# A two-layer DeltaNet and Mamba-2 decode step on one core: regrouped side work, castings in other places, norms by logarithm and exponential

## The reference, cut to what matters

```python
DEPTH = 2    # layer 0: gated DeltaNet (GDN), layer 1: Mamba-2 SSD; D_MODEL = 2048, f32 throughout
for i in range(DEPTH):
    hn = rmsnorm(h, norm_w[i])
    h = h + mixer_i(hn)                   # in-projection, causal conv, SiLU, chunked scan, gate, out-projection
    e = rmsnorm(p[i] @ W_proj_i, ple_norm_w[i])
    h = h + e * sigmoid(h @ W_gate_i)     # "ple"
y = rmsnorm(h, final_norm_w)

def l2norm(x):                            # GDN: on q and k, per head of 128
    return x * rsqrt(sum(x * x) + EPS)
# GDN per head pair: A = I + strict lower part, inverted; u, w, qk; state S (128 x 128) over chunks
# sample tokens, per sequence b: kv = k_t S_b ; o = q_t S_b   ("readout" of the 8 cached states)
# SSD per group: cb = C B^T, y_diag, y_off from the state, S = decay * S + B^T x
```

## Time and profile before

| | |
|---|---|
| median of 3 runs | 2591.24 us (2588.82 to 2592.79) |
| profiled execution, its own time | 2590.68 us |
| its span | 2588.9 us, so 1.8 us lie around it |
| PE, PEld busy | 94%, 87% |
| POOL, DVE, ACT busy | 67%, 58%, 46% |
| mean granted clock of TensorE | 0.98 |

### The profile page before, as it was taken

The page is one execution under the profiler, slowest core; times in us unless marked ns, Lnnn a source line. Parts: engine busy times, 40 slices in busy tenths (PEclk is TensorE's granted clock), DMA queues, the critical chain, the costliest instruction groups (busy, mean ns, idle before and its releaser), DMA issues.

```text
span 2588.9 us, 58121 instructions
## 1 busy us (share of the span) xinstructions
PE 2439.7 (94%) x21088; PEld 2262.6 (87%) x21088; DVE 1491.2 (58%) x2978; ACT 1181.6 (46%) x2116; POOL 1734.7 (67%) x2236
## 2 busy tenths in 40 slices
PE   5999999999999999999998989999999999999887
PEld 4889888888888888889998879988898888899887
DVE  7555665555656556562114457888888888611434
ACT  4444444444444444443334346454545455433433
POOL 4455555555555555556797768877887777889776
PEclk9999999999999999999999989999999999999989
DMA  5344444334333343434443336655576546454433
GB/s 193 137 147 140 145 139 147 123 134 139 127 129 129 139 145 139 139 133 169 147 163 135 136 140 228 230 182 184 199 237 207 184 169 220 176 175 156 141 123 125
DMA packets 126772, 410.83 MB, mean 159 GB/s; under 512 B 21345, under 2 KB 37985, under 8 KB 122113
## 3 DMA queue, kind: packets, MB, share of 16 engines
q1 hardware_dynamic: 81216, 295.75, 33.0%
q10 hardware_dynamic: 45504, 114.38, 13.1%
HBM read 363.47 MB, written 46.61 MB: 158 GB/s over the span
## 4 chain that ended last, share of the span: by engine, by line
POOL 59%; issue 37%; PE 3%; POOLq 1%; DVE 0%; ACT 0%; DVEq 0%; ACTq 0%
POOL wl L327 59%; PE psj L350 1%; PE psj L352 1%; PE psj L351 1%; POOLq L331 0%; POOLq L325 0%; DVE h L1940 0%; DVE arena L1938 0%; ACT L1150 0%; POOLq L327 0%; ACT arena L1125 0%; PE psA L374 0%; ACT arena L1333 0%; DVE arena L1410 0%; DVEq L139 0%
## 5 line engine op out<-in xcount | busy, mean ns | idle before, releaser
L327 POOL TENSOR_TENSOR wl<-ring,wh 128x256 fp32r<-128x256 f32 x2232 | 1734.5, 811 | 832.5 <-ACT wh L801 829.9
L350 PE MATMUL psj<-xh,wh 128*128 128x288 f32 x4400 | 1376.3, 313 | 74.9 <-POOL wl L327 33.7
L351 PE MATMUL psj<-xl,wh 128*128 128x288 f32 x4400 | 1312.7, 298 | 0.0
L352 PE MATMUL psj<-xh,wl 128*128 128x288 f32 x4400 | 1307.5, 297 | 0.0
L350 PEld LDWEIGHTS psj<-xh,wh 128*128 128x128 f32 x4400 | 838.0, 190 | 143.7 <-issue 62.9
L351 PEld LDWEIGHTS psj<-xl,wh 128*128 128x128 f32 x4400 | 840.8, 191 | 5.4 <-issue 4.4
L352 PEld LDWEIGHTS psj<-xh,wl 128*128 128x128 f32 x4400 | 841.9, 191 | 0.0
L801 ACT ACTIVATE wh<-ring 128x1024 fp32r<-128x1024 f32 x558 | 575.2, 1056 | 530.6 <-PE psj L352 464.3
L872 ACT ACTIVATE arena<-psj 128x256 f32<-128x256 f32 x112 | 42.6, 381 | 265.9 <-PE psj L352 265.9
L1766 DVE SCALAR_TENSOR_TENSOR arena<-arena 128x256 f32<-128x256 f32 x144 | 124.2, 902 | 2.6
L1699 DVE TENSOR_TENSOR h<-h,psj 128x288 f32 x32 | 14.5, 454 | 173.7 <-PE psj L352 173.7
(11 more groups left out here) (345 smaller groups left out, 2895.0 us busy)
## 6 DMA issues: line engine op xcount, KB each, us to landing
ring<-weights_d SPq DMA_DIRECT2D x558, 512.0 KB, 3.3
h<-gstate_d ACTq DMA_DIRECT2D x16, 1024.0 KB, 4.8
gst_s_d<-h ACTq DMA_DIRECT2D x16, 1024.0 KB, 4.6
h<-sstate_d ACTq DMA_DIRECT2D x32, 512.0 KB, 5.4
sst_s_d<-h ACTq DMA_DIRECT2D x32, 512.0 KB, 6.0
arena<-g_rows_d ACTq DMA_DIRECT2D x16, 864.0 KB, 4.2
arena<-s_rows_d ACTq DMA_DIRECT2D x8, 1152.0 KB, 8.0
h_spill_d<-h ACTq DMA_DIRECT2D x2, 2304.0 KB, 8.0
```

The lines of the kernel that those rows point to most:

```text
L327: ins = pool.tensor_tensor(wl[:, s, n:n + 2], ring[:, s, n:n + 2], wh[:, s, n:n + 2].bitcast(F32), ALU.subtract)
L350: pe.matmul(out, w_h, xh[:, kt, :], start=(kt == 0), stop=False)
L351: pe.matmul(out, w_h, xl[:, kt, :], start=False, stop=False)
L352: mm = pe.matmul(out, w_l, xh[:, kt, :], start=False, stop=(kt == KT - 1))
```

## The change

It has many parts. In groups:

1. **GDN norms of q and k.** `gdn_norm` sums the squares by a product with ones that leaves the sum on every partition (two matmuls of 288 columns, into psA and psB). ScalarE then takes the logarithm (L912, L913) and the exponential of -0.5 times it (`g_qk_roots`), and VectorE multiplies by that. `gdn_scale` and the reciprocals are gone. The output norm (`OR`) is made in the same way.
2. **Sample work of the GDN heads on four tiles.** The readout writes k and q products of both value heads into four column groups of 32, 128 columns each, where it wrote two groups of 256. `us`, `osm`, `esp`, the copies and norms behind follow that layout.
3. **Fewer breaks.** GDN: `us` joins e = 23, `osm` and `gdn_norm` join e = 27, `esp` goes to e = 15, and the wait for `g_bs` goes from unit 14 to 15. SSD: `s_tok` at 20, chunk state 0 and readout at 32, `s_off`, chunk state 1, `s_smp` and chunk output 0 at 34, chunk output 1 and transposes at 44, states at 49 and 59. That is seven breaks for eleven.
4. **VectorE's order.** The taps of the v convolution are put in smaller pieces between the steps of the inversion. In the SSD group y1 and the state go ahead of the sample chain.
5. **ScalarE's order.** Castings move at the starts of the dense stages. In `ple` a tile is cast one tile earlier, and the squares run one later. In the SSD group the SiLU of the sample columns goes behind `decays(0)`.
6. **The beginning.** Inputs are issued from two queues, and the squares no longer wait for `prm`.

```diff
             def gdn_norm(m):
                 pe.wait_ge(S("g_sq"), m + 1)
-                for n in range(2):
-                    for c in range(NC):
-                        pe.matmul(psB[:, 2 * n + c:2 * n + c + 1], gSQ[:, n, c * CH:(c + 1) * CH], ones[:, 0:1],
-                                  start=True, stop=True)
...
+                for n, bank in enumerate((psA, psB)):
+                    mm = col_sum(bank[:, 0:T], gSQ[:, n, :])
                 mm.then_inc(S("g_ss"), 1)
-            def gdn_scale():
...
                     for b in range(DEC_B):
                         for n in range(2):
-                            mm = pe.matmul(psD[NS * n:NS * n + NS, 0:2 * P], (gMK, gMQ)[n][:, b, :], gS[:, b, :, :],
-                                           start=(b == 0), stop=(b == DEC_B - 1))
+                            for j in range(2):
+                                at = NS * (2 * n + j)
+                                mm = pe.matmul(psD[at:at + NS, 0:P], (gMK, gMQ)[n][:, b, :], gS[:, b, j, :],
+                                               start=(b == 0), stop=(b == DEC_B - 1))
...
+                if e == 32:
+                    pe.wait_ge(S("s_btc"), m + 1)
+                    chunk_state(0)
                     pe.wait_ge(S("s_pr"), m + 1)
...
-            def split_x(src, n, t0):
+            def split_x(src, n, t0, first=False, second=False):
+                if first:
+                    upper(0, 0, 2 * t0 + 2)
                 if t0:
                     act.wait_ge(half_done, 2 * t0)
                 for kt in range(n):
+                    if second and kt == n // 2:
+                        upper(0, 0, 2 * t0 + 3)
                     act.activation(xh[:, kt, :], src(kt), ACT.Copy).then_inc(xh_ready, 1)
...
+            for n in (1, 3):
+                act.dma_start(h[:, 4 * n:4 * n + 4, :], x_in[:, 4 * n:4 * n + 4, :]).then_inc(S(f"x_in{n}"), 16)
...
+                act.activation(gSQ[:, 0, :], psA[:, 0:T], ACT.Ln, bias=eps_c)
+                act.activation(gSQ[:, 1, :], psB[:, 0:T], ACT.Ln, bias=eps_c).then_inc(S("g_nc"), 1)
+            def g_qk_roots(m):
+                act.wait_ge(S("g_nc"), m + 1)
+                act.activation(gSQ[:, :, :], gSQ[:, :, :], ACT.Exp, scale=-0.5).then_inc(S("g_rn"), 1)
...
-                act.activation(ga["OR"], ga["OS"], ACT.Sqrt, bias=eps_c, scale=1.0 / P).then_inc(S("g_rs2"), 1)
+                act.activation(ga["OR"], ga["OS"], ACT.Ln, bias=eps_c, scale=1.0 / P).then_inc(S("g_ol"), 1)
+                act.wait_ge(S("g_ol"), m + 1)
+                act.activation(ga["OR"], ga["OR"], ACT.Exp, scale=-0.5).then_inc(S("g_rs2"), 1)
+                if full:
+                    g_qk_roots(m + 1)
...
             def ple(tp, te, es, hq, hbase, td, end):
                     if i == 7:
                         ahead(0, 0, te)
+                    if i == 13:
+                        upper(0, 0, 2 * te + 2)
...
                 gate(0, 0)
+                ahead(0, 0, te + 3)
                 gate(0, 1)
...
                 decays(0)
+                act.wait_ge(S("s_sconv"), m + 1)
+                act.activation(sCV[:, :, SEQ:T], sCV[:, :, SEQ:T], ACT.Silu).then_inc(S("s_scv"), 1)
                 if full:
                     act.wait_ge(S("s_cv"), m + 1)
                     s_load_pack(m + 1)
                 took(2)
```

More of the change, by code:

```diff
@@ L531, in gdn_mix @@
                         .then_inc(S("g_ks"), 1)
-                if e == 26:
-                    for j in range(2):
-                        mm = pe.matmul(psD[NS:2 * NS, 256 + j * P:256 + (j + 1) * P], gQKS[:, j, :],
-                                       gVNS[:, j * P:(j + 1) * P], start=True, stop=True)
-                    mm.then_inc(S("g_sample_pe"), 1)
                 if e == 27:
@@ L539, in gdn_mix @@
                     new_values(1)
-                if e == 28 and more:
-                    gdn_norm(m + 1)
+                    for j in range(2):
+                        mm = pe.matmul(psD[NS * (2 + j):NS * (3 + j), 256:256 + P], gQKS[:, j, :],
+                                       gVNS[:, j * P:(j + 1) * P], start=True, stop=True)
+                    mm.then_inc(S("g_sample_pe"), 1)
+                    if more:
+                        gdn_norm(m + 1)
                 if e == 29:
@@ L696, in ssd_mix, with chunk_state, chunk_y @@
                     mm.then_inc(S("s_tok"), 1)
-                if e == 27:
+                def chunk_state(c):
+                    pe.wait_ge(S("s_xd"), m * 2 + c + 1)
+                    pe.matmul(psA[:, :], sBT[:, c, :], sa["XD"], start=True, stop=True).then_inc(S("s_s"), 1)
+                def chunk_y(c):
+                    pe.wait_ge(S("s_w"), m * 2 + c + 1)
+                    for i in range(SX):
+                        for j in range(2):
+                            mm = pe.matmul((psB, psC)[c][HD * j:HD * j + HD, i * P:(i + 1) * P],
+                                           sX[:, c, 2 * i + j, :], sDT[:, 2 * i + j, :], start=True, stop=True)
+                    mm.then_inc(S("s_y"), 1)
+                if e == 32:
+                    pe.wait_ge(S("s_btc"), m + 1)
+                    chunk_state(0)
                     pe.wait_ge(S("s_pr"), m + 1)
@@ L705, in ssd_mix @@
                     mm.then_inc(S("s_ro"), 1)
-                if e == 29:
+                if e == 34:
+                    pe.wait_ge(S("s_s1"), m + 1)
+                    for i in range(SX):
+                        mm = pe.matmul(psD[:, i * P:(i + 1) * P], sS1[:, i * P:(i + 1) * P],
+                                       sCV[:, 1, CH:2 * CH], start=True, stop=True)
+                    mm.then_inc(S("s_off"), 1)
+                    chunk_state(1)
                     pe.wait_ge(S("s_roc"), m + 1)
@@ L827, in normed_x @@
                 for kt in range(KT):
+                    if kt == 3 and not t0:
+                        upper(0, 0, 2)
                     if kt == KT // 2:
-                        ahead(0, 0, t_next)
+                        upper(0, 0, 2 * t0 + 3)
                     act.wait_ge(S("xn"), base + kt + 1)
@@ L943, in _ @@
             g_qk_sums(0)
[L944 to L946 removed]
+            g_qk_roots(0)
             decay_rows(GV, "g_")
```

282 lines of the change are left out of this document (123 added, 159 removed).

## The result

The changed kernel takes 2508.67 us as a median (2503.37 to 2511.02), before 2591.41 in the same comparison: a ratio of 0.968, 95% interval 0.9665 to 0.9696. It is faster by 83 us. I had forecast 125 (2466, range 2434 to 2496), so the direction was right, but the gain is a third smaller than forecast and the time lies outside the range. The profiled execution has a span of 2506.0 us for 2588.9.

The account below looks back on a forecast made before the run. The prediction took PE, busy 94% of the span, as the bound. GDN -92, dense starts -34, beginning and SSD start -5 and SSD groups +6 gave -125 from 2590.7, so 2466 us, range 2434 to 2496.

Parts of the forecast that it names:

- GDN heads: GDN loop: shorter readout and sample work, fewer breaks and waits take 5.75 us off each head, 63.6 for 69.34.
- SSD groups: SSD layer: a removed wait and breaks against two new waits, +1.2 us a group in seven, +6 in all.
- stall at unit 32: SSD groups: PE waits 3.0 us for tile 4, cast behind ScalarE's longer chain and then POOL.
- last group: Last SSD group: its castings for O2 come earlier and give 2.5 us.
- dense starts: Starts of dense stages: six `wl` stalls and their lower clock go, additions of +2 and +3 come: -34 us.
- The prologue: GDN prologue: it loses one `gdn_scale` and its reciprocal, -2 us.
- The beginning: Kernel start: first squares no longer wait for `prm` and start some 2.5 us earlier, -3 us.
- The stall of 1.6 at unit 44: SSD groups: chunk output 1 waits 1.6 us for `s_w`, made behind VectorE's sample chain of 10.3 us.
- A: SSD groups: no stall at unit 32, 29 us less, 2437 us; chance 0.2.
- B: GDN readout: four column groups don't run abreast at 128 columns, so it stays at 3.6 us; 2493 us; chance 0.13.
- C: ScalarE: a table switch costs 1.4 us more than its row, total 2492 us; chance 0.04.
- D: GDN heads: ScalarE's longer program makes PE wait in every head beyond 2.4 us cover; slower than before; chance 0.03.

Follow-up runs that it names:

- gdn_only: The kernel before with only the GDN part of the change; dense starts, beginning and SSD groups as before: 2506.88 us.
- ro2: The changed kernel with the GDN heads' readout of cached states on two column groups in place of four: 2535.91 us.
- e_split: On top of `took2`, VectorE's 16 scalings of e cut in two: 4, the first two gated sums of h, then 12: 2447.19 us.
- lower_split: The changed kernel; in the last SSD group 8 of 16 `xl` blocks, then chunk state 1's input, then the other 8: 2502.84 us.
- took2: The changed kernel with the first half of tile 4 cast ahead of chunk 0's decays in each SSD group: 2456.58 us.
- st46: On top of `took2`, the state products of all SSD groups back at units 46 and 57 from 49 and 59: 2471.90 us.
- two_loads: The changed kernel with two more table loads between logarithm and exponential of the output norm in each GDN head: 2527.12 us.
- gate_old: The changed kernel with the casting of E's fourth tile moved behind the first two gates and a wait for new h: 2511.70 us.
- no_i13: The changed kernel with the first half of E's second tile cast ahead of the `xh` blocks, not among the squares: 2511.64 us.
- silu_copy: The changed kernel with the SiLU of the SSD sample columns replaced by a copy, dropping a table load in seven groups: 2485.39 us.

## Why the prediction was right and wrong

The heads were worked out rightly. Two terms failed, and they make most of the 43 us between forecast and result. The SSD groups were put at +6 us and took +28: the lower clock behind the stall at unit 32 had no term, the first group was given a gain that it can't have, and the last group's wait chain was read as a gain. The dense starts were put at -34 and gave -24: POOL's new work was taken to cost VectorE nothing.

- **GDN heads, -5.75 each: right.** Measured -5.58. The readout gave 1.70 (1.6 predicted), `gdn_scale` 1.85 (1.85), the wait for `g_bs` 0.64 (0.64) and a second wait for VectorE, at L1527, 0.23 (0), `us`, `osm` and the transposes 0.63 (0.85), the norm's products 0.23 (0), and the four breaks 0.44 (0.8); other small products took 0.2 more. That breaks gave half of their term and that the sum is right all the same is in part luck. Shown by the trace and by `gdn_only`; the readout by `ro2`.
- **The prologue, -2: wrong.** It lost 0.7. PE waits there for the start of the first head's inversion, which VectorE makes behind ScalarE's decays. Its timeline has it:

```profile
93.57 1.11 PE L423 MATMUL psB<-cst,arena 128*128 128x128 f32 x4 [5.00 <-DVE arena L1498]
```

  Before, the same wait was 2.87 us. `gdn_scale` was hidden: PE is done with what ScalarE copies next at 82.0, but ScalarE is at two castings until 83.6 (before, both ended at 85.1). I gave the term without asking what covers it. The wait has grown by more, since three of VectorE's steps ahead of the inversion took 2.69 us in place of 1.10. VectorE's and POOL's timelines, before:

```profile
89.86 0.68 DVE L1485 TENSOR_TENSOR arena<-arena,cst 128x512 f32<-128x512 f32 x1
90.46 0.21 DVE L1486 TENSOR_TENSOR arena<-arena 32x64 f32<-32x64 f32 x1
...
91.24 3.82 POOL L327 TENSOR_TENSOR wl<-ring,wh 128x256 fp32r<-128x256 f32 x4 [1.32 <-ACT wh L801]
```

  And after:

```profile
87.72 1.31 DVE L1486 TENSOR_TENSOR arena<-arena,cst 128x512 f32<-128x512 f32 x1
88.95 0.73 DVE L1487 TENSOR_TENSOR arena<-arena 32x64 f32<-32x64 f32 x1
...
77.31 14.93 POOL L325 TENSOR_TENSOR wl<-ring,wh 128x256 fp32r<-128x256 f32 x20 [3.05 <-ACT wh L779]
```

  Before, POOL was idle from 89.92 to 91.24, just beside these steps; now it is busy until 92.24. That looks like the effect at E, but no run tried it here.
- **The beginning, -3: half.** The first squares start at 6.03 and no longer at 7.53, 1.5 us earlier, and they now wait 2.37 us for h itself.
- **Dense starts, -34: they gave -24.** The six stalls went, as forecast. Two terms were mis-sized. The lower clock behind the stalls was worth little: the tiles behind the six start 35.5 us earlier, for 32.7 us of stalls (5.2 for 4.21 at the second half of O1, 6.4 for 6.28 at E1), so some 3 us in all and not 6. And I put +2 and +3 for what comes in, where 11 came in. Of these, 2.7 are the longer wait for `xl` at the two starts of E. In the rest the step "POOL needing 3.04 us" looked at POOL alone: with POOL kept busy VectorE's scalings took twice their time, and the gate's wait costs 4 to 5 us in each layer, as `e_split` gave back.
- **SSD groups, +6: they took +28, or +29 with the layer's start.** Unit 32's stall was the right mechanism and too small: 3.83 for 3.0, and 2.3 to 2.9 of lower clock behind it, for which my sum has no term. Before, four of the seven waits at unit 25 had a low spell behind them, of 3.4 us each, and those groups are only 0.5 us longer than the others (83.3 for 82.8). Now the six groups behind the first have one of 6.8 us each, and it lies on the chunk state and the readout. The stall of 1.6 at unit 44 never came. VectorE's sample chain takes 7.2 us, from 1789.93 to 1797.12, and not 10.3. The timelines of VectorE and of POOL:

```profile
1793.67 0.29 DVE L1874 TENSOR_TENSOR arena<-arena 128x128 f32<-128x128 f32 x1
1794.00 0.29 DVE L1876 TENSOR_TENSOR arena<-arena 128x128 f32<-128x128 f32 x1
```

```profile
1786.64 6.13 POOL L325 TENSOR_TENSOR wl<-ring,wh 128x256 fp32r<-128x256 f32 x8 [5.84 <-ACT wh L779]
```

  POOL is idle from 1792.77 on, and each small step takes 0.19 to 0.29 us, where before, beside POOL, it took 0.62 to 0.72. So the absence of what cost at E paid here.
- **The first group.** I took the removed wait at unit 25 seven times. In the trace of before the first group has none, so it had nothing to win and lost 6.9. A count from the rows of all groups would have shown it.
- **The last group, -2.5: wrong by 10.7.** I said that castings for O2 come earlier, and missed that its first projection at unit 32 waits for the same late half, and that `lower_x` stands in front of chunk state 1. Undone one at a time, these give 6.2 us (`lower_split`) and 8.9 (`took2`), and the old place of the state products 4.1 more on top of `took2` (`st46`). Together that is more than the 8.2 lost, so they overlap and can't be added up.
- **The rivals.** A (no stall at 32) didn't come by itself; built by hand (`took2`) it was worth more than the 29 us that I gave it, 52. B is refuted by `ro2`, C by `two_loads` (in the traces a load has 1.28 us and its function starts 10 to 20 ns behind it). D's cover was measured to within a few tenths.

What stays open: SSD start and prologue lost 1.3 us where I had -2. PE's stalls there come behind ScalarE, which waits some 2 us longer than before for the rows written to and read from memory. But the same stretch has 70.7 us in `gate_old` and 72.8 in `no_i13`, which both leave it as it is, so neither the loss nor a gain of 2 us can be told from what it varies by.

## What to carry to other kernels

Before a stall is removed, look at who works undisturbed because of it: an idle POOL may be what makes VectorE fast, and the traces show it at three places here. Price a wait by its length and by the clock behind it, and look at what work lies there. And when a chain of engines feeds the bound one, put the small step that it waits for first (a casting, the first of 16 scalings), since one moved casting was worth 52 us here and one cut in the scalings 9.

## What the runs showed of the hardware

- VectorE with two operands in SBUF and POOL hold each other up, in two ways. In E they alternate: 0.86 us for each of 16 scalings where 0.44 is VectorE's time alone, and 0.90 for POOL's instruction (14.47 for 16) where 0.71 is POOL's (2.82 for 4). In the last group of `took2` VectorE's 16 blocks keep their pace (0.37 us each) and one POOL instruction of 0.7 us takes 8.34: it ends at 2087.59, behind the 16 blocks and the next two instructions of VectorE (2086.99). VectorE's and POOL's timelines of `took2`:

```profile
2080.21 5.98 DVE L1354 TENSOR_TENSOR xl<-Y,xh 128x288 fp32r<-128x288 f32 x16
```

```profile
2079.25 8.34 POOL L325 TENSOR_TENSOR wl<-ring,wh 128x256 fp32r<-128x256 f32 x1 [2.19 <-ACT wh L779]
```

  The Trainium skill, SBUF — State Buffer, section "SBUF: two separate sides", says that the two share a port pair as an exclusive lock, also where the VectorE operation has two SBUF inputs and GpSimd's reads SBUF, as here, and that the loser fully blocks. The trace agrees that POOL can be shut out for the whole of VectorE's burst. It doesn't agree that a lock lasts for all of an instruction's recorded time: by that one of each would take 0.44 + 0.71 = 1.15 us in turn, and they took 0.9. Which of the two ways comes was not tried.
- TensorE's granted clock behind a wait is one of two levels, and the wait's length doesn't decide which. In one kernel (`silu_copy`) a wait of 2.90 us at the same place was followed by none of the lower level in the third group and by a spell of 6.8 us in the seventh, and that group was 2.9 us longer. Behind the waits of 3.83 us the lower level came each time; before the change it came behind four of seven waits of 2.60.
- A table load costs its 1.28 us and 10 to 20 ns, even with three close together.
- Matmuls of 128 columns on four column groups go at 26.7 ns from start to start, on two groups at 54.2 (`ro2`), and those of 256 columns on two groups, before, at 105.4. So on two groups the columns count and not the number of records, down to 128.
